# Memory rows kept unsplit through the experts, their split moved from VectorE to GpSimd, and half of one expert's first matrix loaded into the freed buffer

## The reference, cut to what matters

```python
def hier_moe(xn, w_group, b_group, w_er, b_er, w_e_in, w_e_out):
    g_logits = (xt @ w_group) + b_group
    e_logits = (xt @ w_er) + b_er
    ...
    xs = xt[tok_sorted]
    hdn = lax.ragged_dot(xs, w_e_in, group_sizes)
    gate_h, up_h = jnp.split(hdn, 2, axis=-1)
    act = jax.nn.silu(gate_h) * up_h
    ys = lax.ragged_dot(act, w_e_out, group_sizes)
    ...
def second_block(x, mem, ...):
    mem_n = rmsnorm(mem, mem_norm_g)
    for layer in range(2):
        mem_kv = mem_n @ w_mem_kv[layer]
        ...
```

## Time and profile before

| | |
|---|---|
| median of 3 runs | 1323.81 us (1322.87 to 1324.84) |
| the profiled execution | 1322.58 us |
| its span, first to last instruction | 1320.9 us |
| granted TensorE clock, mean | 0.991 |
| PE busy | 1236.1 us, 94% |
| ACT busy | 659.5 us, 50% |
| POOL busy | 770.3 us, 58% |
| DVE busy | 483.7 us, 37% |
| read from memory | 272.85 MB, 207 GB/s over the span |

### The profile page before, as it was taken

The page is one execution under the profiler, slowest core; times in us unless marked ns, Lnnn a source line. Parts: engine busy times, 40 slices in busy tenths (PEclk is TensorE's granted clock), DMA queues, the critical chain, the costliest instruction groups (busy, mean ns, idle before and its releaser), DMA issues.

```text
span 1320.9 us, 18486 instructions
## 1 busy us (share of the span) xinstructions
PE 1236.1 (94%) x7264; PEld 988.4 (75%) x7264; DVE 483.7 (37%) x1084; ACT 659.5 (50%) x1148; POOL 770.3 (58%) x345
## 2 busy tenths in 40 slices
PE   8999999999888778999899999999999889999998
PEld 6888877777343333888788888888998678888986
DVE  2527343433121111456603444102458281344411
ACT  6455544653111011745646666545798443666651
POOL 5778985440000000982176888996688905788894
PEclk8999999998999999999999999999999999999999
DMA  6745554298999999562143655653534413355561
GB/s 210 259 138 187 191 186 159 100 366 334 422 421 375 422 422 413 177 221 81 33 150 113 206 181 184 237 190 128 191 128 169 167 65 128 129 191 192 191 204 67
DMA packets 127037, 275.01 MB, mean 208 GB/s; under 512 B 6580, under 2 KB 55020, under 8 KB 115180
## 3 DMA queue, kind: packets, MB, share of 16 engines
q1 hardware_dynamic: 126668, 272.86, 56.6%
q10 hardware_dynamic: 288, 1.05, 0.2%
HBM read 272.85 MB, written 1.05 MB: 207 GB/s over the span
## 4 chain that ended last, share of the span: by engine, by line
PE 75%; DMA 8%; ACT 7%; DVE 4%; POOL 3%; issue 2%; SPq 1%; DVEq 0%; ACTq 0%; POOLq 0%
PE lin_ps L950 11%; PE lin_ps L952 11%; PE lin_ps L951 11%; DMA ring<-in_w_expert_in 7%; PE lin_ps L1003 6%; PE sc_ps L1268 4%; POOL w_low L877 3%; PE lin_ps L1005 3%; PE tr_ps L1003 3%; PE sc_ps L1003 3%; PE lin_ps L980 2%; PE lin_ps L983 2%; PE lin_ps L982 2%; ACT w_high L1568 2%; PE lin_ps L1088 2%
## 5 line engine op out<-in xcount | busy, mean ns | idle before, releaser
L877 POOL TENSOR_TENSOR w_low<-ring,w_high 128x1024 fp32r<-128x1024 f32 (+1 forms) x318 | 761.0, 2429 | 456.0 <-ACT w_high L1568 456.0
L1568 ACT ACTIVATE w_high<-ring 128x1024 fp32r<-128x1024 f32 (+1 forms) x320 | 313.8, 1043 | 102.1 <-PE lin_ps L952 32.7
L950 PE MATMUL lin_ps<-w_high,x_span 128*128 128x512 f32 (+2 forms) x432 | 168.6, 390 | 5.1 <-POOL w_low L877 2.6
L951 PE MATMUL lin_ps<-w_low,x_span 128*128 128x512 f32 (+2 forms) x432 | 166.2, 385 | 0.0
L952 PE MATMUL lin_ps<-w_high,x_low 128*128 128x512 f32 (+2 forms) x304 | 116.5, 383 | 0.0
L1003 PE MATMUL lin_ps<-x_span,w_high 128*128 128x512 f32 x320 | 112.6, 397 | 1.5 <-ACT work L1598 1.5
L950 PEld LDWEIGHTS lin_ps<-w_high,x_span 128*128 128x128 f32 x432 | 81.7, 189 | 21.8 <-DVE w_low L2115 2.8
L951 PEld LDWEIGHTS lin_ps<-w_low,x_span 128*128 128x128 f32 x432 | 81.8, 189 | 15.2
L980 PE MATMUL lin_ps<-x_span,w_high 128*128 128x256 f32 x320 | 91.4, 286 | 0.0
L982 PE MATMUL lin_ps<-x_span,w_low 128*128 128x256 f32 x320 | 90.5, 283 | 0.0
L1005 PE MATMUL lin_ps<-x_span,w_low 128*128 128x256 f32 x320 | 89.3, 279 | 0.0
(11 more groups left out here) (465 smaller groups left out, 2371.7 us busy)
## 6 DMA issues: line engine op xcount, KB each, us to landing
ring<-in_w_expert_in SPq DMA_DIRECT2D x30, 2048.0 KB, 16.0
ring<-in_ffn_w_in SPq DMA_DIRECT2D x44, 1024.0 KB, 7.4
ring<-in_w_in SPq DMA_DIRECT2D x12, 2048.0 KB, 7.8
ring<-in_b_w_in SPq DMA_DIRECT2D x11, 2048.0 KB, 8.1
work<-in_w_expert_out SPq DMA_DIRECT2D x8, 2048.0 KB, 23.3
ring<-in_w_expert_out SPq DMA_DIRECT2D x8, 2048.0 KB, 22.4
ring<-in_ffn_w_out SPq DMA_DIRECT2D x8, 2048.0 KB, 7.8
ring<-in_a_w_in SPq DMA_DIRECT2D x4, 2048.0 KB, 8.0
```

The source lines that it names most:

```text
L877: pool.tensor_tensor(w_low[:, slot, 0:words], raw, w_high[:, slot, 0:words].bitcast(F32), ALU.subtract).then_inc(low_made, 1)
L950: pe.matmul(out[:, t, :], high(k)[:, at], wh[:, j, :], start=(k == 0), stop=False)
L951: pe.matmul(out[:, t, :], high(k)[:, at], wl[:, j, :], start=False, stop=False)
L1568: act.activation(w_high[:, slot, 0:words], raw, ACT.Copy).then_inc(high_made, 1)
```

## The change

The memory rows stay one f32 matrix in buffer 6 (`mem_T`): ScalarE copies them out of PSUM with their gain, raises `x_low_made` itself, and VectorE's eight low parts go. TensorE's wait for all eight stands amid w_out1 (when k is 2) instead of ahead of it. GpSimd makes the high part (now in buffer 9) and the low part (over `mem_T`, in buffer 6) after batch 1 has used both halves of its first matrices, and TensorE waits for that (`mem_split`) before kv00. Until then buffer 9 is free: the a=1 half (1 MB) of batch 1's first expert is loaded there ahead, and the load that brought that half with the next expert's becomes one of half the size. The filler can no longer multiply the high part; it multiplies `ident`, an f32 matrix of 128x128, by itself, 64 and 26 times.

```diff
+        later_slot = buf(9).rearrange("p (k n) -> p k n", k=4)
+        def first_matrix(extra, a, e, k):
+            if extra and a == 0:
+                return extra_slot(e)[k // 2][:, k % 2, :]
+            if extra and e == 0:
+                return later_slot[:, k, :]
+            return first_slot(a)[:, e, k, :]
...
+                sp.wait_ge(x_low_made, split_groups["merged"] + 8)
+                sp.dma_start(later_slot, io["w_expert_in"][0][BATCH].rearrange("(p k) n -> p k n", k=KC)[:, 4:8, :])\
+                    .then_inc(extra_in, 16)
                 last_use(3)
                 load_first(0, 1, 1)
...
-                firsts_when_free(1, 1, 1)
+                sp.wait_ge(expert_used[1], 1)
+                sp.dma_start(first_slot(1)[:, 1], io["w_expert_in"][0][BATCH + 1].rearrange("(p k) n -> p k n", k=KC)[:, 4:8, :])\
+                    .then_inc(expert_in[1], 16)
+                load_first(1, 1, 1)
...
             pool.wait_ge(expert_used[0], 2)
+            pool.wait_ge(expert_used[1], 2)
+            step(pool.tensor_copy(mem_high[:], mem_T))
+            pool.tensor_tensor(mem_low[:], mem_T, mem_high[:].bitcast(F32), ALU.subtract).then_inc(mem_split, 1)
...
             turn_split("mem", 8, scaled_mem)
-            parts_made(pe, "mem", 8)
...
                 if k == 2:
+                    parts_made(pe, "mem", 8)
                     pe.wait_ge(h_half, TILES)
...
-                    pe.matmul(lin_out("w_out1")[:, 0, 0:SEQ], mem_high[:, i % KC, 0:P], mem_high[:, i % KC, :], start=True, stop=True)
-            keep_running(34)
+                    pe.matmul(lin_out("w_out1")[:, 0, 0:P], ident[:], ident[:], start=True, stop=True)
+            keep_running(64)
...
-            keep_running(14)
+            keep_running(26)
...
+            pe.wait_ge(mem_split, 1)
             linear_turned("kv00", *from_mem)
...
-            take_high(act, "mem", 8, mem_high, "mem")
+            for i in range(KC):
+                act.wait_ge(x_turned, split_groups["mem"] + i + 1)
+                act.activation(mem_T[:, i, :], split_ps(i), ACT.Copy, scale=col("mem", i)).then_inc(x_low_made, 1)
+            act.sem_inc(x_high_made, KC)
...
-                    take_low(dve, "mem", 8, mem_high, mem_low, "mem")
```

More of the change, by code:

```diff
@@ L261, in program @@
         x_low4, x_low5 = (overlay(f"x_low{i}", 2048 * i, [P, KC, SEQ]) for i in (4, 5))
-        mem_high, mem_low = overlay("mem_high", 6 * 2048, [P, KC, SEQ]), overlay("mem_low", 9 * 2048, [P, KC, SEQ])
+        mem_high, mem_low = overlay("mem_high", 9 * 2048, [P, KC, SEQ]), overlay("mem_low", 6 * 2048, [P, KC, SEQ])
         cat_high, cat_low = overlay("cat_high", 4 * 2048, [P, 12, SEQ]), overlay("cat_low", 7 * 2048, [P, 12, SEQ])
@@ L399, in program @@
         router_done = sem("router_done")
+        mem_split = sem("mem_split")
         moe_pick = sem("moe_pick")
@@ L495, in program @@
         scaled_mem = tok(buf(8))
+        mem_T = feat(buf(6))
         km_T = [feat(buf(7, 1024)), feat(buf(5, 1024, 1024))]
@@ L1262, in expert_batch @@
                     if extra and a == 0:
-                        pe.wait_ge(extra_in, 16 * 2 * BATCH)
+                        pe.wait_ge(extra_in, 16 * (2 * BATCH + 1))
                     else:
@@ L1269, in expert_batch @@
                                            gathered[:, 4 * a + k, CAP * e:CAP * (e + 1)],
-                                           extra_slot(e)[k // 2][:, k % 2, :] if extra and a == 0 else first_slot(a)[:, e, k, :],
+                                           first_matrix(extra, a, e, k),
                                            start=(a == 0 and k == 0), stop=(a == 1 and k == 3))
```

## The result

The changed kernel takes **1335.08 us** (median of 5 runs, 1333.3 to 1337.32); the kernel before takes 1323.81 beside it (5 runs, 1321.05 to 1327.38). The ratio is 1.0088, 95% interval [1.0072, 1.0104]: slower by 11.3 us, where 11.9 were forecast. The profiled execution of the changed kernel is its longest run, 1337.32 us with a span of 1335.6, so the two profiles lie 14.7 us apart (1335.6 against 1320.9).

A forecast was written before the change was run, and what follows sets the result against it. TensorE's chain was taken as the bound, except the experts' last four batches, paced by the load queue. Terms -2.5 + 10.3 + 4.1 = +11.9 us, others 0, gave 1335.7 us against the median 1323.81; range 1331 to 1341.

The forecast's parts named there:

- The split taken off VectorE, -2.5: Memory rows' transposes: only ScalarE's copies gate them, so w_out1 and all up to the filler start 2.5 us earlier.
- The first filler, +10.3: Filler before the selection: 128 f32 passes, 23 at half clock and 105 at 0.112 us, 16.7 us against 6.38.
- the second, +4.1: Filler before the picks: 52 f32 passes at 0.112 us, 5.8 us against 1.76.
- the first rival: Filler passes cost only their columns, half as much: fillers +3.1 and +1.2, time 1325.6 us; chance 0.05.
- The clock left where it was: TensorE's half-clock stretch, from near 307.8 to 314.7 us, stays in place, with 4.95 us of it in the first filler.
- the forecast's lower bound (no fall): Clock never falls around router and filler, passes at 0.104 us: +7.0, or 1331 us.
- The megabyte, 0: Batch 1's early 1 MB load takes 2.5 us off the later queue, which then only runs dry earlier: 0.
- The dry stretch at the first gap: Load queue near the first expert product: idle until TensorE releases a slot, about 17 us in the changed kernel.
- The second gap: Load queue before batch 3's slot release, around 401 us in the kernel before: dry for some 6 to 7 us after the change.
- Everything behind shifts whole: Expert stage: a later first batch moves the slot releases, both queue restarts and the stage's end by as much.
- The split on GpSimd, 0: GpSimd's copy and subtraction after batch 1, 7 to 10 us, fit its idle time before kv00: 0.
- the slowing that was held open: VectorE slowed by a busy GpSimd during the split, from 0 to 2.9 us; taken as 0.

The follow-up runs named there:

- old_filler: The changed kernel with the filler of before (34 and 14 fp32r products, made on merged_low) instead of the new one: 1320.56 us, 0.9978 of the kernel before.
- wait_moved_alone: The kernel before with only TensorE's wait for the memory rows' eight parts moved amid w_out1; VectorE still makes the low parts: 1320.83 us, ratio 0.998.
- old_filler_no_megabyte: As old_filler, but the half matrix of batch 1's first expert is loaded in its old place, without the early 1 MB transfer: 1318.87 us, ratio 0.9974.
- new_filler_alone: The kernel before with nothing changed but the filler, now 64 and 26 products on ident: 1337.37 us, ratio 1.01.
- trimmed_filler: As old_filler, but with 26 and 6 filler products instead of 34 and 14: 1322.17 us, 0.9985 of the kernel before.
- no_filler: The changed kernel without any filler product: 1324.34 us, 1.0005 of the kernel before.
- half_filler: The changed kernel with 32 and 13 products on ident instead of 64 and 26: 1323.02 us, 0.9995 of the kernel before.
- fp32r_128_columns: The changed kernel with its 64 and 26 filler products of the same shape on fp32r operands instead of f32: 1333.11 us, 1.0044 of the kernel before.

## Why the prediction was right

**Direction and size.** 1335.7 forecast, 1335.08 measured, inside 1331 to 1341.

**The split taken off VectorE, -2.5.** Right. The filler starts 308.40 - 286.23 = 22.17 us after the transposes, against 309.72 - 285.02 = 24.70 before: -2.5. old_filler has it without the new filler. By wait_moved_alone some 1.4 of it need only the wait to be moved; the other 1.3 need VectorE's parts out of the transposes' way (1.4 and 1.3 are more than 2.5 because the router's products ran slower in the profile after, 2.96 us against 2.74).

**The first filler, +10.3, and the second, +4.1.** 16.57 against 6.38 is +10.2, and 5.89 against 1.76 is +4.1. The count was right (180 entries of L1254 for 90 products), and so was the price: 5.89/52 = 0.113 us. The 0.212 that was taken from the opening for half clock holds too: the passes of this filler start 0.213 us apart where the clock reads 0.50. (The 1.00 of the opening has nothing behind it: the trace's first entry on the clock stands at 7.5 us.) That row of 5.89 is also the answer to the first rival. The Trainium skill, "TensorE: Matmul & The Clock Gate", section "Wait — 56ns, not 53.3ns?", has 55.6 ns for 128 columns at the full clock; the f32 passes of 128 columns, each with its own weight load, took 0.113 here, and fp32r ones were profiled at half clock alone (0.214). That no wait hides the filler shows in VectorE's timeline of the changed kernel: the selection's mask is made at 313.08, and VectorE then stands idle for TensorE's placing.

```profile
313.08 0.23 DVE L2352 TENSOR_TENSOR work<-work 128x64 f32<-128x64 f32 x1
...
326.11 0.22 DVE L2358 TENSOR_TENSOR work<-work,sc_ps 128x64 f32<-128x64 f32 x1 [12.58 <-PE sc_ps L1262]
```

**The clock left where it was.** Right for this profile: the windows of the changed kernel show 0.71 from 310 to 315 us and 1.00 from then on. The stretch at half clock is as long as before (6.8 us), and 4.5 us of it lie in the filler, where 4.95 were forecast.

```profile
310.00:315.00 5.00, 5.00 (x35) 5.00 (x34) 3.09 (x19) 2.35 (x6) 0.00 (x0) 0.71 1.01 424
315.00:320.00 5.00, 5.00 (x47) 5.00 (x46) 0.00 (x0) 0.00 (x0) 0.00 (x0) 1.00 1.02 419
...
326.00:342.00 16.00, 15.44 (x143) 11.29 (x146) 4.17 (x15) 2.95 (x3) 0.00 (x0) 1.00 0.09 22
...
410.00:415.00 5.00, 5.00 (x52) 1.62 (x48) 0.00 (x0) 0.00 (x0) 0.00 (x0) 1.00 0.26 66
```

But it was luck that the two profiles agree. Of the ten profiles of the experiments one has 6.8 us at half clock between the transposes and the first expert product, one 3.4, one 13.7, one 27.3 and six none; the forecast's lower bound (no fall) might as well have come.

**The megabyte, 0.** Right, shown by old_filler_no_megabyte. Two sizes were off. The dry stretch at the first gap lasts some 14.6 us (16 us with a share of 0.09, the window of 326 to 342), not 17, since the megabyte also keeps the queue busy for longer ahead of the gap (new_filler_alone, which lacks it and starts the experts 0.75 us later, has 18.6 us idle there by windows of 1 us, the changed kernel 14.9). The second gap comes to 4.0 us (3.7 in 410 to 415 and 0.3 in the next 5), not 6 to 7. Added up as above from 350 us on, the queue is idle for 5.0 us in the changed kernel and 2.9 before, so most of the megabyte's 2.5 us is there, 0.6 of it in front of the gap, at 389 to 392. Neither size enters the sum.

**Everything behind shifts whole.** Right: E to K is 207.4 to 208.0 in all ten kernels that leave batch 4's loads alone, for first products between 318.69 and 337.00. It rests on a queue that runs dry ahead of the first release. By windows of 1 us that gap holds 14.9 us of idle queue in the changed kernel, 5.7 before, 0.7 in old_filler and 0.1 in trimmed_filler, so experts that start much earlier than those of trimmed_filler may find a full queue, and the shift need not hold for them; no run goes there.

**The split on GpSimd, 0.** Right. Its timeline in the changed kernel:

```profile
367.85 1.89 POOL L920 CAST mem_high<-work 128x2048 fp32r<-128x2048 f32 x1 [88.06 <-PE sc_ps L1289]
369.82 4.55 POOL L921 TENSOR_TENSOR mem_low<-work,mem_high 128x2048 fp32r<-128x2048 f32 x1
```

6.4 us, under the 7 to 10 forecast: the cast is cheaper than its lower bound of 2.1. It ends at 374.4, and the next use is kv00 at 543.94. VectorE's operation at 368.16, beside it, took 0.42 us (L2398), as the same one did before (L2374); the slowing that was held open does not show in this one operation, the only one beside the pair.

## What to carry to other kernels

Filler that keeps TensorE's clock up is work on the critical path like any other: size it by the entries and durations the trace shows for the same shape and type, not by the number of calls, and let it end about when the awaited engine is done; none at all (no_filler) and much more than that (the change) were both slower here than the old one. Bytes loaded ahead pay only if they cross the queue while it would have been idle, and only up to the idle time that is left. Before a buffer is freed for a new use, ask what else reads it: here the loss came from a filler that needed new operands, not from the move itself.

## What the runs showed of the hardware that was not expected

A TensorE pass that loads 128x128 weights of its own cost nearly the same here from 32 to 256 columns. At full clock it is 0.104 us for 32 columns and 0.107 for 36, 0.112 to 0.115 for 128 in f32, and 0.126 for 256 in fp32r (1.76/14); at half clock passes start 0.213 us apart, 128 columns in f32 and in fp32r and 256 in fp32r alike. A pass of the large products, with 512 columns, takes 0.24. So a new pass of half the columns was no cheaper than an old one, and there were 180 of them in place of 48.

A busy TensorE does not always get its clock back: over 21 us of back-to-back work, 19.3 of them fp32r passes of 128 columns, the granted clock stayed at 0.50, while in the changed kernel it came back to 1.00 some 4.5 us into the f32 passes on ident. Both are single profiles, and the cause is open.

Whether and how long the clock falls after about 305 us differs between the profiles, from no time at half clock to 27.3 us. It differs between runs of one kernel too, as far as the mean clock tells (0.990 to 0.997 in half_filler, 0.983 to 0.997 in fp32r_128_columns). A stretch of 6.8 us costs some 2 us: M to G is 31.16 in old_filler with it and 29.14 in old_filler_no_megabyte without. Differences of that size between two profiles of this kernel say nothing until the stretch is compared at the same clock.
